# A small gate chain two tiles later, a cleared buffer moved into a loop step, and attention scores of two heads at a time

## The chip, the cores and the metric

The kernel runs on one core of one Trainium2 chip. The metric is the device time of one execution in microseconds. TensorE (PE in the profile) multiplies matrices into PSUM; VectorE (DVE), ScalarE (ACT) and GpSimd (POOL) work on the data between the multiplications; SyncE (SP) issues most transfers. Each engine runs its own list of instructions in order, and the lists meet at semaphores: an instruction can raise one, and another engine waits until it has reached a number.

## The reference

Two transformer blocks over 256 tokens of width 1024, with a context of 256 more tokens. All is float32. Cut to what the change touches:

```
# block 1, layer 0: gated delta rule on h @ w_in (q, k, v after a convolution), plus a gated MLP
log_alpha = -exp(a_log) * softplus(alpha_raw + dt_bias)      # per token, direction, head
gcum      = cumsum(log_alpha within a chunk)
decay     = exp(gcum_i - gcum_j), a_mat = strict_tril((beta k) k^T * decay)
t_mat     = inverse(I + a_mat)      # u = t_mat @ (beta v), w = t_mat @ (beta k exp(gcum)), then a scan

# block 1, layer 1: multi-head latent attention, 8 heads, 512 keys (256 of context, 256 own)
s = qn_h @ kn_h^T + qr_h @ kr^T     # 128 wide per head, and 64 wide with rotary, kr shared
p = softmax(s * 192**-0.5);  o_h = p @ v_h;  y = concat(o) @ w_out
```

Other layers (a convolutional MLP, a second block with three more attentions) are not changed.

## The kernel before

**Weights and tiles.** All weights pass through one stream of blocks of 128 x 1024. A block is split into a high and a low part: ScalarE makes the high one (`split`, line 1563), VectorE the low one (`low`, line 2060), and PE multiplies high x high, high x low and low x high (`mm3`, lines 646 to 648). A tile (`tile`) is 24 matmuls of 512 columns in this stage and 256 later. Two PSUM banks (PL[0], PL[1]) alternate for its results; six more (BK[0] to BK[5]) serve the small products. In the input stage block n is tile n; step t of ScalarE and VectorE handles block t + 2, and ScalarE can split block t + 2 only when PE has ended tile t (two buffers). Beside it, VectorE multiplies the rows of the modulation weights (`mod_tile`, line 2191, two passes of 1024 elements a step).

**The gate chain.** Tile 12 holds the raw gates of all tokens. From step 12 on, a chain goes through four engines, each step of it written by hand at a given step t of each engine's loop `for t in range(GATES, 25)`:
- ScalarE, t = 12 (`gate_rows`): bias, sigmoid, abs, exp and log on 8 rows, then the logarithm of the lengths of q and k (L2, read from BK[4], `l2_log`).
- VectorE, t = 13: gate rows (lines 2230, 2231, `g_soft`). PE, after tile 13: four transposes (line 778).
- VectorE, t = 14: copy to GTOK (line 2234, `g_tok`). PE, after tile 14: cumulative sums into BK[5] (lines 786, 787, `g_cs`).
- VectorE, t = 15: log factors (lines 2239 to 2248, `g_cum`). ScalarE, t = 15: exponential (line 1716, `g_exp`).
- PE, after tiles 15 and 16: `key_products` of the first stream's two token tiles (lines 768, 769; the second writes BK[4] and BK[5]).
- VectorE, t = 16: factors times beta (lines 2252, 2253, `g_fac`), for which PE waits after its second key products.
- After tiles 17, 19, 21, 23 (`ROWS_AT`): `rows` on PE (lines 760, 761), `decays` (2207) and `triangles` (2215 to 2222) on VectorE, two exponentials on ScalarE (1696, 1699), and a product on GpSimd (`decayed`, 1456). `rows` of one q waits until the triangles and exponentials before it are done.

**The inverse.** After the loop come 28 steps k for each of the two streams (`LEVELS`: 7 levels x 4 quarters). A step is a masked block on GpSimd (line 1476, `lev_ct`), a first product on PE (893 or 900), a copy on ScalarE (1770), a second product (917, 920) and a subtraction on VectorE (2351 to 2364). VectorE starts it with `first_u` (2330), after its last low part. Before the steps GpSimd clears the buffer TU (line 1461) when all modulation products of the stage are done; TU is first written by VectorE at the sixth level. At k = 8, 9, 10 GpSimd also issues three small transfers.

**The first attention** (`attend` with the layer MLA) has 16 items, head h and query tile qt. PE's step a is: scores of item a into one of three banks, transposes of item a - 2 (line 1140), values of item a - 3 (line 1189, into BK[4 + h % 2]). The scores are one product of all 128 rows of the array (line 1184) and one rotary product of 64 rows (line 1185), rows 0 to 63 for even heads and 64 to 127 for odd ones. A float32 product shows as two matmul instructions. VectorE's step is: reduce and scale item a, normalise item a - 1, and after every second item (`per` = 2, `lag` = 5) the low part of a finished head. ScalarE's step is: exponential of item a, copy of the transposes of item a - 2, high part of a finished head. The projection `out1` follows and takes the heads as its eight chunks.

Of the kernel before, what the change touches and what calls it, by code (L numbers as in the profile page):

```python
# [24 lines left out]
P = 128  # L25
# [259 lines left out]
def two_blocks_kernel(nc, x_in, mem_in, a_head, a_stream, cond_rows, w_stream, cols, gdn_tables, late_tables, ident, ws_t, bs_row, ln_rows, w_uk, w_uv, out):  # L285
# [4 lines left out]
    with ctx:  # L290
# [240 lines left out]
        class Layer:  # L531
            def __init__(self, name, heads, key_tiles, per_group, a0, e0, scale):
                self.name, self.heads, self.kt, self.per, self.a0, self.e0 = name, heads, key_tiles, per_group, a0, e0
                self.n, self.scale = 2 * heads, scale
                self.banks = [BK[0], BK[1], PL[0]]
                self.lag = per_group + 3
                self.steps = self.n - per_group + self.lag + 1
# [9 lines left out]

        MLA = Layer("mla", 8, 4, 2, 0, 0, 192 ** -0.5)
        DIL = PairLayer("dil", 16, 8, 64 ** -0.5)
        DSA = PairLayer("dsa", 24, 10, 96 ** -0.5)  # L550
        CRS = Layer("cross", 4, 2, 2, 32, 12, 256 ** -0.5)
        LAT = slice(SEQ, T2)
# [47 lines left out]
        GATES, UV_AT, GATE_AT = 12, 13, 21  # L600
        ROWS_AT = {17: 0, 19: 1, 21: 2, 23: 3}

# [39 lines left out]
        def _(pe):  # L642
# [130 lines left out]
            for t in range(GATES, 25):  # L773
                tile(t, t, slice(0, T2), T2)
                if t == 13:
                    pe.wait_ge(G["g_soft"], 1)
                    for x in range(4):
                        last = nc.tensor.transpose(BK[0][:, 40 * x:40 * x + 40], GT[0:40, x * P:(x + 1) * P], ID[0:40, 0:40])
                    last.then_inc(G["g_tr"], 1)
                if t == 14:  # L780
                    pe.wait_ge(G["g_tok"], 1)
                    pe.wait_ge(gdn_in, 16)
                    for d in range(2):
                        o = BK[5][:, 0:64].rearrange("p (t d r) -> p t d r", t=4, d=2)[:, :, d, :]
                        g = GTOK[:, :, 4 * d:4 * d + 4]
                        mm(o[:, :, 0:4], gtab("cum", d), g, start=True, stop=True)
                        last = mm(o[:, :, 4:8], ONES[:], g, start=True, stop=True)
                    last.then_inc(G["g_cs"], 1)
                if t == 15:
                    pe.wait_ge(silu_done, 8)  # L790
                    key_products(0, 0)
                if t == 16:
                    pe.wait_ge(G["g_cum"], 1)
                    key_products(0, 1)
                    pe.wait_ge(G["g_fac"], 1)
                if t in ROWS_AT:
                    rows(0, ROWS_AT[t])
# [70 lines left out]
            for st in range(2):  # L868
                if st:
# [8 lines left out]
                pe.wait_ge(G["gb_at"], 4 * st + 3)  # L878
                pe.wait_ge(G["gb_e"], 14 if st else 8)
# [247 lines left out]
            def attend(ly, scores, values):  # L1127

                nb = len(ly.banks)
                for a in range(ly.n + 3):  # L1130
                    if a < ly.n:
                        if ly.a0 or a >= nb:

                            pe.wait_ge(A["at_p"], ly.a0 + max(0, a - nb + 1))
                        scores(a // 2, a % 2, ly.banks[a % nb]).then_inc(A["at_s"], 1)
                    if 2 <= a < ly.n + 2:
# [5 lines left out]
                    if a >= 3:  # L1142
# [3 lines left out]
                        if p % ly.per == 0 and ly.e0 + e >= 2:  # L1146
                            pe.wait_ge(A["at_y"], ly.e0 + e - 1)
                        values(p // 2, p % 2, PT[:, p % 2, :, :]).then_inc(A["at_o"], 1)

# [31 lines left out]

            def mla_scores(h, qt, o):
                q, po = slice(qt * P, (qt + 1) * P), 64 * (h % 2)
                mm(o[:], MQ[:, h, q], KN[:, h, :], start=True, stop=False)
                return mm(o[:], MQ[po:po + 64, 8 + h // 2, q], KR[po:po + 64, :], start=False, stop=True)  # L1185

            def mla_values(h, qt, pt):
                for k in range(4):
                    last = mm(BK[4 + h % 2][:, qt * P:(qt + 1) * P], VT[:, k, h * P:(h + 1) * P], pt[:, k, :], start=(k == 0), stop=(k == 3))  # L1189
                return last  # L1190

            attend(MLA, mla_scores, mla_values)
            project("out1", LAT, SEQ, lambda k: (A["at_y"], k + 1))
            norm("n2_1")
# [229 lines left out]
        def _(pool):  # L1424
# [33 lines left out]
            for q in range(4):  # L1458
                decayed(0, q)
            pool.wait_ge(m_acc, 2 + 2 * MOD_IN)  # L1460
            nc.gpsimd.memset(TU[:], 0.0).then_inc(G["u_zero"], 1)
            for st in range(2):
# [3 lines left out]
                for k, (lev, q) in enumerate(LEVELS):  # L1466
# [79 lines left out]
        def _(act):  # L1546
# [154 lines left out]
            for t in range(GATES, 25):  # L1701
# [12 lines left out]
                if t == 15:  # L1714
                    act.wait_ge(G["g_cum"], 1)
# [188 lines left out]
            def attend(ly, out_bank, out_chunks):  # L1904
                for a in range(ly.steps):
                    w = ly.kt * P
                    if a < ly.n:
                        r = a % 3
                        act.wait_ge(A["at_m"], ly.a0 + a + 1)
                        if ly.a0 + a >= 3:  # L1910
                            act.wait_ge(A["at_t"], ly.a0 + max(0, a - 2))
                        f(PB[:, r, 0:w], ly.banks[r][:, 0:w], ACT.Exp, scale=STD[:, 10 + a % 2:11 + a % 2] if ly is CRS else ly.scale, bias=SM[:, 20 + r:21 + r], accum_out=SM[:, 24 + r:25 + r]).then_inc(A["at_p"], 1)
                    if 2 <= a < ly.n + 2:
# [38 lines left out]

            attend(MLA, lambda e: BK[4 + e % 2][:, 0:SEQ], lambda h, e: h[:, e, LAT])
            residuals("out1", 1, "n2_1")
# [90 lines left out]
        def _(dve):  # L2045
# [179 lines left out]
            for t in range(GATES, 24):  # L2225
                low(t + 2)
                if t == 13:
# [4 lines left out]
                if t == 14:  # L2232
                    dve.wait_ge(G["g_tr"], 1)
                    v.tensor_copy(GTOK[:], BK[0][:, 0:160].rearrange("p (t r) -> p t r", t=4)).then_inc(G["g_tok"], 1)
                if t == 15:
                    cum, total = GC[:, :, :, 0:4], GC[:, :, :, 4:8]
# [4 lines left out]
                    dve.wait_ge(G["g_cs"], 1)  # L2241
                    link(v.tensor_copy(GC[:], BK[5][:, 0:64].rearrange("p (t d r) -> p t d r", t=4, d=2)))
                    v.tensor_tensor(RP[:], cum, by_q, ALU.add)
# [4 lines left out]
                    v.tensor_tensor(BR, by_k, by_q, ALU.subtract).then_inc(G["g_cum"], 1)  # L2248
                if t == 16:
                    beta = GTOK[:, :, 32:40].rearrange("p t (d h) -> p t d h", d=2)  # L2250
# [284 lines left out]
            def attend(ly, out_bank, out_chunks):  # L2535
                for a in range(ly.steps):
                    w = ly.kt * P
                    if a < ly.n:
                        r = a % 3
                        dve.wait_ge(A["at_s"], ly.a0 + a + 1)  # L2540
                        link(v.tensor_reduce(SM[:, 16 + r:17 + r], ly.banks[r][:, 0:w], AXES.X, ALU.max))
                        if ly is CRS:
# [33 lines left out]

            attend(MLA, lambda e: BK[4 + e % 2][:, 0:SEQ], lambda h, e: h[:, e, LAT])
            project("out1", SEQ, 8)
# [146 lines left out]
```

## Time and profile before

| | |
|---|---|
| median of 3 runs | 1704.24 us (1702.66 to 1706.44) |
| profiled execution, whole | 1709.05 us |
| its span (first to last instruction) | 1707.2 us |
| mean granted PE clock | 0.96 |
| busy: PE, DVE, ACT, POOL | 1585.0 (93%), 1142.9 (67%), 787.8 (46%), 115.0 (7%) |
| chain that ended last, by engine | PE 79%, DVE 11%, ACT 5%, issue 3% |
| DMA | 230.50 MB, mean 135 GB/s |

The profile is of one execution, and its times run from the start of its span. Busy time of PE is modelled: a matmul's shown time reaches past the start of the next one, so the spacing of starts is the time that it costs. "Idle before" is time in which an engine stood still ahead of an instruction, with the instruction that released it. A row with "x8" merges eight instructions.

### The profile page before, as it was taken

What the parts mean: (1) busy time and instruction counts of PE and PEld (TensorE: products, weight loads), DVE (VectorE), ACT (ScalarE), POOL (GpSimd) and SP (SyncE); (2) the same over time, 40 slices, a digit from 0 to 9 for tenths busy, and PEclk for the clock granted to TensorE, in tenths of its full rate; (3) what the DMA queues carried; (4) which work ended last, traced back from release to release, by engine and by line L of the source; (5) the groups of instructions that cost most, each with busy time, mean ns of one, the idle gap of its engine ahead of it and who ended that gap; (6) DMA issues with size and microseconds to landing.
All of it is one profiled execution on the core that took longest, in us unless ns stands there. A gap on an engine that the chain in (4) does not pass through costs nothing.

```text
span 1707.2 us, 30981 instructions
## 1 busy us (share of the span) xinstructions
PE 1585.0 (93%) x11422; PEld 1387.1 (81%) x11422; DVE 1142.9 (67%) x1917; ACT 787.8 (46%) x1421; POOL 115.0 (7%) x130
## 2 busy tenths in 40 slices
PE   5997978889999999999999999999999988999998
PEld 2786868788777777788787589999898768999997
DVE  5974755554499999967455558885565665477653
ACT  3644533132354544432256447775444445566532
POOL 2000032220200000001000010001000001010000
PEclk9998988898999999999999999999899999999999
DMA  8343330000245555554432034556443222355552
GB/s 352 128 172 117 131 118 3 1 3 1 99 136 184 184 184 185 185 181 165 147 119 87 25 99 148 184 186 214 162 166 136 99 75 87 112 173 184 185 189 94
DMA packets 62906, 230.50 MB, mean 135 GB/s; under 512 B 6816, under 2 KB 8096, under 8 KB 62304
## 3 DMA queue, kind: packets, MB, share of 16 engines
q1 hardware_dynamic: 61408, 223.37, 38.4%
q0 software_dynamic: 1120, 5.54, 1.0%
q8 instruction: 64, 1.05, 0.3%
q10 hardware_dynamic: 288, 0.33, 0.1%
q14 instruction: 26, 0.21, 0.0%
HBM read 228.17 MB, written 1.05 MB: 134 GB/s over the span
## 4 chain that ended last, share of the span: by engine, by line
PE 79%; DVE 11%; ACT 5%; issue 3%; POOL 1%; DMA 1%; DVEq 0%; ACTq 0%; POOLq 0%
PE proj L646 21%; PE proj L648 20%; PE proj L647 20%; DVE w_low L2060 2%; PE bank L698 1%; ACT w_high L1563 1%; PE bank L900 1%; PE bank L917 1%; PE bank L1189 1%; PE bank L920 1%; DVE conv_mid L2140 1%; PE bank L1185 1%; PE proj L1101 1%; DMA ident_sb<-ident 1%; PE bank L948 1%
## 5 line engine op out<-in xcount | busy, mean ns | idle before, releaser
L646 PE MATMUL proj<-h_high,w_high 128*128 128x256 f32 (+1 forms) x1768 | 585.0, 331 | 23.2 <-DVE h_low L2093 14.0
L648 PE MATMUL proj<-h_high,w_low 128*128 128x256 f32 (+1 forms) x1768 | 572.2, 324 | 0.0
L647 PE MATMUL proj<-h_low,w_high 128*128 128x256 f32 (+1 forms) x1768 | 571.8, 323 | 0.0
L2060 DVE TENSOR_TENSOR w_low<-w_raw,w_high 128x1024 fp32r<-128x1024 f32 x322 | 393.3, 1224 | 197.9 <-ACT w_high L1563 196.5
L1563 ACT ACTIVATE w_high<-w_raw 128x1024 fp32r<-128x1024 f32 x322 | 338.1, 1054 | 251.7 <-PE proj L648 246.3
L646 PEld LDWEIGHTS proj<-h_high,w_high 128*128 128x128 f32 x1768 | 337.3, 191 | 65.9 <-issue 18.1
L648 PEld LDWEIGHTS proj<-h_high,w_low 128*128 128x128 f32 x1768 | 337.6, 191 | 27.3
L647 PEld LDWEIGHTS proj<-h_low,w_high 128*128 128x128 f32 x1768 | 337.3, 191 | 25.5
L646 PE MATMUL proj<-act_high,w_high 128*128 128x256 f32 (+1 forms) x608 | 190.1, 313 | 0.4 <-DVE w_low L2060 0.4
L647 PE MATMUL proj<-act_low,w_high 128*128 128x256 f32 (+1 forms) x608 | 189.9, 312 | 0.0
L648 PE MATMUL proj<-act_high,w_low 128*128 128x256 f32 (+1 forms) x608 | 188.9, 311 | 0.0
L646 PEld LDWEIGHTS proj<-act_high,w_high 128*128 128x128 f32 x608 | 114.1, 188 | 8.5 <-DVE w_low L2060 0.8
L648 PEld LDWEIGHTS proj<-act_high,w_low 128*128 128x128 f32 x608 | 114.3, 188 | 7.4
L647 PEld LDWEIGHTS proj<-act_low,w_high 128*128 128x128 f32 x608 | 113.9, 187 | 6.6
L1642 ACT ACTIVATE conv_in<-proj 128x512 f32<-128x512 f32 (+1 forms) x100 | 49.8, 498 | 120.5 <-PE proj L648 117.5
L2191 DVE SCALAR_TENSOR_TENSOR mod_products<-a_ring,cond_rows 128x1024 f32<-128x1024 f32 x80 | 103.0, 1287 | 0.1
L1441 POOL TENSOR_TENSOR tmp<-tmp 128x256 f32<-128x256 f32 (+1 forms) x40 | 43.7, 1099 | 806.3 <-ACT tmp L1579 627.9
L2191 DVE SCALAR_TENSOR_TENSOR a_ring<-a_ring,cond_rows 128x1024 f32<-128x1024 f32 x80 | 97.6, 1220 | 0.0
L2142 DVE SCALAR_TENSOR_TENSOR conv_mid<-conv_in,cols_sb,conv_mid 128x512 f32<-128x512 f32 (+1 forms) x100 | 63.5, 635 | 14.0 <-DVE conv_mid L2140 8.2
L2140 DVE SCALAR_TENSOR_TENSOR conv_mid<-conv_in,cols_sb,conv_mid 128x512 f32<-128x512 f32 (+1 forms) x100 | 63.3, 633 | 12.1 <-ACT conv_mid L1643 9.7
L1643 ACT ACTIVATE conv_mid<-proj,cols_sb 128x512 f32<-128x512 f32 (+1 forms) x100 | 58.8, 588 | 0.0
L1770 ACT ACTIVATE lev_m<-bank 128x256 f32<-128x256 f32 (+1 forms) x48 | 18.3, 383 | 84.6 <-PE bank L900 71.8
(406 smaller groups left out, 1939.2 us busy)
## 6 DMA issues: line engine op xcount, KB each, us to landing
w_raw<-w_stream SPq DMA_DIRECT2D x322, 512.0 KB, 3.3
a_ring<-a_stream SPq DMA_DIRECT2D x80, 512.0 KB, 3.2
a_first<-a_head SPq DMA_DIRECT2D x4, 1024.0 KB, 17.9
a_first<-a_stream SPq DMA_DIRECT2D x4, 1024.0 KB, 18.5
x<-x_in SPq DMA_DIRECT2D x1, 2048.0 KB, 10.6
late_tab<-late_tables POOLq DMA_DIRECT2D x1, 1408.0 KB, 6.6
cond_rows<-cond_rows SPq DMA_DIRECT2D x1, 1024.0 KB, 5.9
cond_rows<-cond_rows POOLq DMA_DIRECT2D x1, 1024.0 KB, 5.0
```

The source lines that it names most:

```text
L646: mm(out_, wh, xh, start=first, stop=False)
L647: mm(out_, wh, xl, start=False, stop=False)
L648: return mm(out_, wl, xh, start=False, stop=last)
L1441: nc.gpsimd.tensor_tensor(squares(name, 0), squares(name, 0), squares(name, k), ALU.add).then_inc(n_early, 1)
L1563: f(wh(n), RAW[:, n % 4, :], ACT.Copy).then_inc(w_high, 1)
L1642: f(XP[:, k % 2, 0:n, 1:SEQ + 1], PL[t % 2][:, 0:width].rearrange("p (s t) -> p s t", s=n), ACT.Copy)
L1643: f(C1[:, k % 2, 0:width], PL[t % 2][:, 0:width], ACT.Identity, scale=C[:, ds(taps + 3 * k + 1 + 3 * per * it, 1)]).then_inc(tile_out, 1)
L1770: f(M1[x, k % 2, :, :], BK[k % 2][x, 0:4 * 64].rearrange("p (h j) -> p h j", h=HEADS), ACT.Copy).then_inc(G["lv_m1"], 1)
L2060: v.tensor_tensor(wl(n), RAW[:, n % 4, :], wh(n), ALU.subtract).then_inc(w_low, 1)
L2140: v.scalar_tensor_tensor(o, XP[:, k % 2, 0:n, 0:SEQ], C[:, ds(taps + 3 * k + 3 * per * it, 1)], o, ALU.mult, ALU.add).then_inc(conv_mid, 1)
L2142: v.scalar_tensor_tensor(o, XP[:, k % 2, 0:n, 2:SEQ + 2], C[:, ds(taps + 3 * k + 2 + 3 * per * it, 1)], o, ALU.mult, ALU.add).then_inc(con ...
L2191: v.scalar_tensor_tensor(o, w, 1.0, cond[:, s, :], ALU.mult, ALU.mult, accum_out=MODF[:, ds(2 * (A_FIRST + j) + s + 2 * off, 1)]).then_inc ...
```

## The change

Three edits.

1. PE's key products come after tiles 13 and 14 (the second waits for `l2_log`, since it writes the bank that ScalarE reads the lengths from). The transposes come after tile 15, the sums after tile 16 (now in BK[1]), the wait for the factors after tile 18; the rows after 18, 20, 22 and 23. VectorE's gate rows are at t = 14, its copy at 16, its log factors at 17, its products with beta at 18; ScalarE's exponential at 17. Before the first stream's inverse PE waits for all four triangles, not three.
2. GpSimd clears TU at k = 8 of the first stream's inverse.
3. The attention MLA takes two heads' scores for one query tile in an even step: four full-height instructions, then the rotary ones of both heads. It has four score banks (PL[1] added); items are ordered head, head + 1 for one query tile, then for the other; outputs leave in groups of four items (`per` = 4, `lag` = 7) as 512 columns for two heads, and the later counts (`e0`) follow.

```diff
-        ROWS_AT = {17: 0, 19: 1, 21: 2, 23: 3}
+        ROWS_AT = {18: 0, 20: 1, 22: 2, 23: 3}
...
                 if t == 13:
+                    pe.wait_ge(silu_done, 8)
+                    key_products(0, 0)
+                if t == 14:
+                    pe.wait_ge(G["l2_log"], 1)
+                    key_products(0, 1)
+                if t == 15:
                     pe.wait_ge(G["g_soft"], 1)
...
-                if t == 14:
+                if t == 16:
                     pe.wait_ge(G["g_tok"], 1)
...
-                if t == 15:
-                    pe.wait_ge(silu_done, 8)
-                    key_products(0, 0)
-                if t == 16:
-                    pe.wait_ge(G["g_cum"], 1)
-                    key_products(0, 1)
+                if t == 18:
                     pe.wait_ge(G["g_fac"], 1)
...
-            pool.wait_ge(m_acc, 2 + 2 * MOD_IN)
-            nc.gpsimd.memset(TU[:], 0.0).then_inc(G["u_zero"], 1)
...
                     if st == 0 and k == 8:
+                        pool.wait_ge(m_acc, 2 + 2 * MOD_IN)
+                        nc.gpsimd.memset(TU[:], 0.0).then_inc(G["u_zero"], 1)
...
-        MLA = Layer("mla", 8, 4, 2, 0, 0, 192 ** -0.5)
+        MLA = Layer("mla", 8, 4, 4, 0, 0, 192 ** -0.5)
...
-                        if ly.a0 or a >= nb:
+                        if ly is MLA and a % 2 == 0:
+                            if a >= nb:
+                                pe.wait_ge(A["at_p"], a - nb + 2)
+                            scores(a, ly.banks[a % nb:a % nb + 2])
...
+            def mla_scores(a, banks):
+                h, qt = a // 4 * 2, a // 2 % 2
+                q = slice(qt * P, (qt + 1) * P)
+                for i, o in enumerate(banks):
+                    mm(o[:], MQ[:, h + i, q], KN[:, h + i, :], start=True, stop=False)
+                for i, o in enumerate(banks):
+                    mm(o[:], MQ[HALVES[i], 8 + h // 2, q], KR[HALVES[i], :], start=False, stop=True).then_inc(A["at_s"], 1)
```

## Rows read from the trace of the kernel before

**Rows 1.** Timeline of PE: start us, us, instruction [idle us before <- released by], its four waits.
```profile
140.81 0.65 PE L778 MATMUL bank<-ident_sb,gate_t 40*128 40x40 f32 x4 [6.75 <-DVE gate_t L2231]
...
151.31 0.57 PE L786 MATMUL bank<-g_tok,gdn_tab 128*128 128x16 f32 x2 [2.70 <-DVE g_tok L2234]
...
171.15 0.50 PE L646 MATMUL proj<-h_high,w_high 128*128 128x512 f32 x1 [0.88 <-DVE factors L2253]
...
227.04 4.01 PE L893 MATMUL bank<-ident_sb,lev_ct 64*64 64x64 f32 x64 [4.47 <-POOL lev_ct L1476]
```

**Rows 2.** Two windows: length, busy PE, granted clock, DMA share, GB/s.
```profile
151.30:158.20 6.90, 6.89 (x20) 0.51 0.41 152
...
250.40:253.40 3.00, 3.00 (x64) 0.50 0.02 5
```

**Rows 3.** Timeline of PE: first and second key products, tile 16 between them.
```profile
161.01 0.39 PE L768 MATMUL bank<-qkv 128*128 128x128 f32 x2
...
162.72 0.48 PE L646 MATMUL proj<-h_high,w_high 128*128 128x512 f32 x1
...
168.31 0.39 PE L768 MATMUL bank<-qkv 128*128 128x128 f32 x2
```

**Rows 4.** Timelines of ScalarE and VectorE: lengths' logarithm, copy of g_tok, factors.
```profile
137.17 0.29 ACT L1707 ACTIVATE qk_lengths<-bank,cols_sb 128x32 f32<-128x32 f32 x1
...
150.94 0.32 DVE L2234 COPY g_tok<-bank 128x160 f32<-128x160 f32 x1
...
170.91 0.18 DVE L2253 TENSOR_TENSOR factors<-factors,g_tok 128x32 f32<-128x32 f32 x1
```

**Rows 5.** Timelines of VectorE and GpSimd around the start of the inverse.
```profile
221.97 1.23 DVE L2191 SCALAR_TENSOR_TENSOR mod_products<-a_ring,cond_rows 128x1024 f32<-128x1024 f32 x1
...
224.72 1.22 DVE L2060 TENSOR_TENSOR w_low<-w_raw,w_high 128x1024 fp32r<-128x1024 f32 x1
226.93 1.27 DVE L2330 TENSOR_TENSOR inv_u_halves<-gdn_tab,lev_ct 128x256 f32<-128x256 f32 x2 [0.99 <-POOL lev_ct L1476]
...
224.40 1.80 POOL L1461 MEMSET inv_u<- 128x2048 f32 x1 [3.16 <-DVE a_ring L2191]
...
236.59 0.59 POOL L1482 DMA_DIRECT2D ln_rows_sb<-ln_rows  x1
241.77 0.72 POOL L1476 TENSOR_TENSOR lev_ct<-a_halves,gdn_tab 128x256 f32<-128x256 f32 x1 [4.58 <-PE bank L900]
```

**Rows 6.** Timeline of PE: first attention's start, one step of it, the projection behind it.
```profile
939.34 1.12 PE L1184 MATMUL bank<-mla_k,mla_q 128*128 128x512 f32 x2 [1.31 <-DVE kr L2528]
...
952.95 1.02 PE L1184 MATMUL proj<-mla_k,mla_q 128*128 128x512 f32 x2
953.90 1.12 PE L1185 MATMUL proj<-kr,mla_q 64*128 64x512 f32 x2
954.96 0.66 PE L1140 MATMUL bank<-ident_sb,probs 128*128 128x128 f32 x4
...
956.34 1.02 PE L1184 MATMUL bank<-mla_k,mla_q 128*128 128x512 f32 x2
...
994.81 0.36 PE L646 MATMUL proj<-h_high,w_high 128*128 128x256 f32 x1
```

**Rows 7.** Line 1185 (rotary products): ns minimum/median/maximum, first and last start.
```profile
L1185 PEld LDWEIGHTS bank<-kr,mla_q x22: 182/184/186, 940.4 to 987.9; 64*128 64x128 f32 x22
L1185 PE MATMUL bank<-kr,mla_q x22: 589/641/693, 940.4 to 988.4; 64*128 64x512 f32 x22
```

**Rows 8.** Timeline of PE: index scores (L1228, halves alternate), dilated scores (L1211, one half).
```profile
1315.72 0.70 PE L1228 MATMUL bank<-proj 64*128 64x256 f32 x4
...
1335.75 1.13 PE L1211 MATMUL bank<-proj 64*128 64x256 f32 x4
```

**Rows 9.** Groups by line, 939 to 995: busy us, mean ns | idle before.
```profile
L2541 DVE TENSOR_REDUCE small<-bank 128x1 f32<-128x512 f32 x11 | 7.6, 692 | 13.3 <-PE bank L1185 13.3
...
L1912 ACT ACTIVATE probs<-bank,small 128x512 f32<-128x512 f32 x11 | 7.6, 687 | 21.7 <-DVE small L2545 21.7
```

More of the change, by code:

```diff
@@ L534, in __init__ @@
                 self.n, self.scale = 2 * heads, scale
-                self.banks = [BK[0], BK[1], PL[0]]
+                self.banks = [BK[0], BK[1], PL[0]] if name == "cross" else [BK[0], BK[1], PL[0], PL[1]]
                 self.lag = per_group + 3
@@ L546, in __init__ @@
                 self.pairs = [(0, 4), (1, 5), (2, 6), (3, 7)] if name == "dsa" else [(0, 2), (1, 3), (4, 6), (5, 7)]
[L548 to L551 removed]
+        MLA = Layer("mla", 8, 4, 4, 0, 0, 192 ** -0.5)
+        DIL = PairLayer("dil", 16, 4, 64 ** -0.5)
+        DSA = PairLayer("dsa", 24, 6, 96 ** -0.5)
+        CRS = Layer("cross", 4, 2, 2, 32, 8, 256 ** -0.5)
         LAT = slice(SEQ, T2)
@@ L1131, in attend @@
                     if a < ly.n:
-                        if ly.a0 or a >= nb:
+                        if ly is MLA and a % 2 == 0:
+                            if a >= nb:
+                                pe.wait_ge(A["at_p"], a - nb + 2)
+                            scores(a, ly.banks[a % nb:a % nb + 2])
+                        elif ly is not MLA:
                             pe.wait_ge(A["at_p"], ly.a0 + max(0, a - nb + 1))
-                        scores(a // 2, a % 2, ly.banks[a % nb]).then_inc(A["at_s"], 1)
+                            scores(a // 2, a % 2, ly.banks[a % nb]).then_inc(A["at_s"], 1)
                     if 2 <= a < ly.n + 2:
@@ L1147, in attend @@
                             pe.wait_ge(A["at_y"], ly.e0 + e - 1)
-                        values(p // 2, p % 2, PT[:, p % 2, :, :]).then_inc(A["at_o"], 1)
+                        h, qt = (p // 4 * 2 + p % 2, p // 2 % 2) if ly is MLA else (p // 2, p % 2)
+                        values(h, qt, PT[:, p % 2, :, :]).then_inc(A["at_o"], 1)
             def pair_step(ly, a, scores, values):
@@ L1180, in pair_step @@
                     last.then_inc(A["at_o"], 1)
[L1182 to L1185, printed above, removed]
+            def mla_scores(a, banks):
[5 more added lines that the diff above has]
+                    mm(o[:], MQ[HALVES[i], 8 + h // 2, q], KR[HALVES[i], :], start=False, stop=True).then_inc(A["at_s"], 1)
             def mla_values(h, qt, pt):
+                at = h % 2 * SEQ + qt * P
                 for k in range(4):
-                    last = mm(BK[4 + h % 2][:, qt * P:(qt + 1) * P], VT[:, k, h * P:(h + 1) * P], pt[:, k, :], start=(k == 0), stop=(k == 3))
+                    last = mm(BK[4 + h // 2 % 2][:, at:at + P], VT[:, k, h * P:(h + 1) * P], pt[:, k, :], start=(k == 0), stop=(k == 3))
                 return last
             attend(MLA, mla_scores, mla_values)
-            project("out1", LAT, SEQ, lambda k: (A["at_y"], k + 1))
+            project("out1", LAT, SEQ, lambda k: (A["at_y"], k // 2 + 1))
             norm("n2_1")
@@ L1911, in attend @@
                             act.wait_ge(A["at_t"], ly.a0 + max(0, a - 2))
-                        f(PB[:, r, 0:w], ly.banks[r][:, 0:w], ACT.Exp, scale=STD[:, 10 + a % 2:11 + a % 2] if ly is CRS else ly.scale, bias=SM[:, 20 + r:21 + r], accum_out=SM[:, 24 + r:25 + r]).then_inc(A["at_p"], 1)
+                        f(PB[:, r, 0:w], ly.banks[a % len(ly.banks)][:, 0:w], ACT.Exp, scale=STD[:, 10 + a % 2:11 + a % 2] if ly is CRS else ly.scale, bias=SM[:, 20 + r:21 + r], accum_out=SM[:, 24 + r:25 + r]).then_inc(A["at_p"], 1)
                     if 2 <= a < ly.n + 2:
@@ L2226, in _ @@
                 low(t + 2)
-                if t == 13:
+                if t == 14:
                     dve.wait_ge(G["g_in"], 1)
@@ L2540, in attend @@
                         dve.wait_ge(A["at_s"], ly.a0 + a + 1)
-                        link(v.tensor_reduce(SM[:, 16 + r:17 + r], ly.banks[r][:, 0:w], AXES.X, ALU.max))
+                        link(v.tensor_reduce(SM[:, 16 + r:17 + r], ly.banks[a % len(ly.banks)][:, 0:w], AXES.X, ALU.max))
                         if ly is CRS:
```

18 lines of the change are left out of this document (9 added, 9 removed).

## The prediction

> **What bounds the kernel now.** I read the page first: TensorE (PE) is busy for 93% of the span and makes up 79% of the chain that ended last, so a change pays where PE waits, runs at the low clock, or has work that can go away. Then I read PE's waits in the timeline of the two stretches that the diff touches. From the end of input tile 13 to the first level product of the scan PE waits four times: 6.8 us for the gate rows before the transposes, 2.7 us for g_tok before the cumulative sums, 0.9 us for the factors before tile 17, and 4.5 us for GpSimd's first masked block [rows 1]. The granted clock comes next: after the 2.7 us wait it is 0.51 for 6.9 us, the lower level (1.2 GHz), and after another wait of 2.6 us elsewhere 0.50 for 3.0 us [rows 2]. In the first attention there is no wait to remove: PE repeats the same step every 3.39 us (952.95 to 956.34) without a gap, so only its own work counts there, 55.47 us from 939.34 to 994.81 [rows 6].
>
> **Change 1, the gate chain two tiles later.** PE's own work in the stretch stays: eleven tiles, four groups of rows, two groups of key products, four transposes, four sums. From 162.72 to 168.31 a tile is 5.59 us at the high clock, and from 161.01 to 162.72 a group of 16 small matmuls 1.71 us [rows 3]. What moves is where PE meets the other engines.
> - Before the transposes (6.75 us now). VectorE made the gate rows after weight block 15, whose split ScalarE could only do after its own gate work. The key products come forward to steps 13 and 14. The first needs only conv outputs made long before. Tile 13 ended at 134.06 (140.81 less 6.75) [rows 1], so they run to 135.8, tile 14 to 141.4, the second group to 143.1, tile 15 to 148.7. The second group waits for the logarithm of the lengths, which ScalarE started at 137.17 for 0.29 us [rows 4]: over by then. The gate rows wait only for block 16, whose split starts when tile 14 ends: about 145. So this wait goes, cover 3.7 us. Nothing is late behind it.
> - Before the sums (2.70 us). This one stays. The copy of g_tok stands on VectorE behind the low part of the block two tiles on, and that block can only be split once PE has ended the tile just run. The rows show it: tile 14 ends at 148.61 (151.31 less 2.70), the copy ran from 150.94 for 0.32 us [rows 1, 4]. At step 16 the same order holds: 2.7 us again.
> - Before the factors (0.88 us). The factors were ready at 171.09 (170.91 plus 0.18), 2.8 us after tile 16 had given way to the key products at 168.31 [rows 3, 4]. Those products covered 1.7 us of it. They are gone from this place, and nothing replaces them: with the tail of the last matmul counted as busy, 2.7 us are exposed at step 18. This edit loses 1.8 us by itself.
> Waits: 6.75 + 2.70 + 0.88 = 10.3 now, 2.7 + 2.7 = 5.4 after: 4.9 us less.
> - Clock. From 140.81 to 148.61 PE needed 7.8 us for transposes and a tile worth 6.0 (5.59 and an estimate of 0.4 for the transposes and switches); from 151.31 to 161.01 9.7 us for sums and a tile worth 6.4 (5.59 + half of the sums' 1.70): 5.1 us lost to the low clock. After: the first wait should repeat the loss that follows it now, 3.3. The second is bounded by the two windows: half of 3.4 us (the 3.0 of the row and its edges) up to half of 6.9, or nothing if the clock holds. I take 1.7, since dense products follow it. Loss 5.0, a gain of 0.1; ends +5.1 and -1.8.
> The stretch gives 5.0 us, ends 3.1 and 10.0. Rows now come at 18, 20, 22 and 23; the third and fourth have only one tile between them. The fourth waits for the third's triangles, which end 6.9 us after a tile's end (the modulation pass behind them starts at 221.97, and tile 23 ended at about 215.1, that is 222.57 less 1.71 less 5.59, less tails) [rows 3, 5]; the rows and the tile between take 7.3 us, so I cost it at nothing, with 0.4 us of cover. If the cover fails, PE stalls by the difference.
>
> **Change 2, clearing the half-block buffer in step 8.** GpSimd now clears it from 224.40 for 1.80 us, after the last modulation product, and VectorE then stands idle 0.99 us for the first masked block [rows 5]. In step 8 the clearing lies between 236.59 plus 0.59 and the next masked block at 241.77 [rows 5]: 4.6 us of GpSimd's waiting hide 1.8. Without that cover it would cost at most 1.8. VectorE's split of block 26 beside today's clearing took its usual 1.22 us, so I expect no slowing of the neighbour. With the clearing gone, the first two masked blocks and products can run before VectorE is free. But VectorE gets later: step 22's two modulation products and block 25 now stand before step 23's decays, by my working about 0.7 us. Today it is free at 225.9 (224.72 + 1.22), 3.4 us after tile 24's end at 222.57; then at 4.1, against 4.4 with the wait for GpSimd. The four first products run 4.0 us at the low clock [rows 1]; two of them leave the path, less the masked block that the third waits for. I take 1.0 us of gain, between -0.7 (VectorE's lateness alone) and 2.5 (two products and the head start).
>
> **Change 3, scores of two heads at a time.** A step now is 0.95 us of full-height products (952.95 to 953.90), 1.06 of half-height rope products, and 1.38 of transposes and values [rows 6]. A pair's four full-height instructions take 1.81 (0.43 each, one change of arrangement instead of two). Its four rope instructions use both halves of the array and two banks. Nothing in this attention shows that; the index scores do: four instructions on alternating halves take 0.70 us, four of equal width on one half 1.13 [rows 8], so they run two by two (the busy time runs 0.17 us past the point at which the next operation starts: 0.53 against 0.96). For 512 columns that makes 1.06 a pair instead of 2.12. PE's work per pair falls from 6.79 to 1.81 + 1.06 + 2.76 = 5.63.
> Not all of it is kept. VectorE's order is reduce(a), then normalise(a-1). The odd item's normalising stands behind the reduce of the next pair, which starts only after all eight score instructions. The reduce takes 0.69, ScalarE's exponential, which goes before the transposed copy, 0.69 [rows 9]; the small operations and handovers come to that. Laid out item by item, PE waits 0.2 us for the odd transposes and 0.3 us for the values in each pair (6.16 a pair), 1.1 us at the start and 1.0 at the end. The stretch comes to 50.7 us; the same laying out gives 55.4 for the kernel before (55.47 in the trace). Gain 4.7. The wider copies (one for two heads) are behind the last values: the projection has 30 matmuls before it needs chunks 6 and 7, so they are hidden; uncovered, they cost 1.5. Ends: 2.2 if the rope products don't overlap, 9.2 if no wait appears (8 x 1.16).
>
> The Trainium skill speaks against the size: "TensorE: Matmul & The Clock Gate", Part 3, section on the mechanism, says that matmuls start and end in strict program order and only weight loads of another row group run ahead. By it the second head's first product could not start before the first head's second, and the four would take about 1.5 us. The trace disagrees (0.70 against 1.13 above) [rows 8]. The sum would hardly move: the reduce comes earlier for the first head, the waits shrink, and the stretch comes to 50.9.
>
> **The sum.** 5.0 + 1.0 + 4.7 = 10.7 us. The profiled execution took 1709.05 (span 1707.2), 4.8 above the median of the runs shown; taken off it, 1698.3, and off the median of 1704.24, 1693.5. The rest is the same work with the same waits.
>
> **Rivals.**
> - The clock holds through both 2.7 us waits. The loss of 5.0 goes, 1688.5. For it: the 0.9 us wait had no low clock behind it. Against: both waits of this size in rows 2 had one. 15%.
> - The attention gives less: the rope products run one after another. Then 2.2 instead of 4.7, 1696. For it: the operands are accumulated here, in the index scores they are not. 12%.
> - The change doesn't do what it says: the wait at the transposes is not the gate rows' lateness but comes back whole two tiles on, or at step 18 and 23, with its clock. Then the stretch gives 0, 1698.5. For it: two of three waits do come back. Against: the 6.75 came from ScalarE's gate work, which is done once, at 137. 7%.
> - Slower: each rope instruction empties the array before the next, since the half changes within a pair. One alone takes 0.69 us, and its weight load 0.18 [rows 7]; four then take 3.5, a pair 1.81 + 3.5 + 2.76 = 8.1 instead of 6.79, eight pairs 10.2 more. With the other 6.0 gained: 1708.4. It decides the sign once the four take over 4.02 - 1.81 + 6.0/8 = 2.96 us. Against: four on alternating halves took 0.70 us in the index scores [rows 8]. 3%.
> My forecast has 63%.
>
> **The numbers.** 1693.5 is the likeliest. Downwards the clock rival (1688.5) and the upper end of the attention reach to about 1686.5; upwards the rivals at 1696 and 1698.5 to 1699.5. About what a measurement of this kernel can tell from no change is 0.2%, 3.4 us. Only the slower rival, and a return of the waits together with a weak attention, miss that: faster 0.93, same 0.04, slower 0.03.
>
> **What would show it.** PE's waits after the change: none at the transposes, one of 2.7 us for g_tok after tile 16, one of about 2.7 for the factors after tile 18, a low clock behind each; the rows after tile 23 without a wait; GpSimd's masked blocks 0 and 1 before VectorE's block 26 has ended; the clearing between masked blocks 8 and 9 with PE's products unmoved. In the attention: pairs every 6.2 us, four rope instructions in 1.1, waits of 0.2 and 0.3 on normalise and on the transposed copy. I am wrong if the waits at steps 16 and 18 are absent or over 4 us, if the rope four take over 1.5, or if tile 24 or the first products wait longer than now.

## The result, and the profile after

The changed kernel took 1694.11 us (median of 5 runs, 1690.71 to 1695.20) against 1704.12 for the kernel before (5 runs, 1700.29 to 1706.44): ratio 0.9934, 95% interval 0.9916 to 0.9952. Forecast: 1693.5, range 1686.5 to 1699.5. Its profiled execution has a span of 1692.0 us, 15.2 less than the 1707.2 of before; only 11.6 of these lie in the code that the change touches.

I cut every span at the same places: the end of input tile 13, the end of tile 24, the first value transposes of the scan, the first score product of the first attention, and the first product of the projection behind it [rows 6]. Us:

| stretch | before | after | after, second profile |
|---|---|---|---|
| start to tile 13's end | 134.1 | 135.5 | 134.2 |
| tiles 14 to 24, with the gate chain | 88.5 | 81.8 | 81.8 |
| start of the scan | 8.4 | 8.0 | 8.0 |
| scan and projections (unchanged code) | 708.4 | 707.9 | 706.5 |
| first attention | 55.5 | 50.9 | 50.9 |
| to the end (unchanged code) | 712.4 | 707.9 | 712.1 |

The timeline of PE after, tile 14 to the scan (start us, us, instruction, in brackets the idle time before it and who ended it), answers [rows 1]:

```profile
150.00 0.43 PE L784 MATMUL bank<-ident_sb,gate_t 40*128 40x40 f32 x4
...
158.84 0.56 PE L792 MATMUL bank<-g_tok,gdn_tab 128*128 128x16 f32 x2 [2.70 <-DVE g_tok L2242]
...
176.87 0.49 PE L760 MATMUL bank<-ident_sb,log_rows 128*128 128x128 f32 x2 [2.67 <-DVE factors L2261]
...
217.99 1.15 PE L894 MATMUL bank<-ident_sb,lev_ct 64*64 64x64 f32 x32 [0.69 <-ACT gate L1721]
...
223.40 1.97 PE L894 MATMUL bank<-ident_sb,lev_ct 64*64 64x64 f32 x32 [4.26 <-POOL lev_ct L1483]
```

No wait at the transposes, one of 2.70 and one of 2.67: all three are as forecast. The 0.69 us ahead of the first two level products, ended by ScalarE (line 1721), is new; the next two products wait for VectorE and GpSimd all the same. The two windows behind them (length; busy us and instructions of PE, PEld, DVE, ACT and POOL; granted clock, DMA share, GB/s) answer [rows 2]:

```profile
158.80:165.70 6.90, 6.86 (x20) 5.79 (x21) 2.27 (x4) 0.00 (x0) 0.00 (x0) 0.51 0.44 163
176.80:189.70 12.90, 12.83 (x64) 10.89 (x65) 9.40 (x19) 5.81 (x7) 1.29 (x1) 1.00 0.36 135
```

The lower level (1.2 GHz) behind the first, none behind the second. VectorE and GpSimd at the end of tile 24 (217.30), which answer [rows 5]:

```profile
217.60 1.75 DVE L2199 SCALAR_TENSOR_TENSOR mod_products<-a_ring,cond_rows 128x1024 f32<-128x1024 f32 x1
...
220.87 1.22 DVE L2068 TENSOR_TENSOR w_low<-w_raw,w_high 128x1024 fp32r<-128x1024 f32 x1
222.01 0.75 DVE L2338 TENSOR_TENSOR inv_u_halves<-gdn_tab,lev_ct 128x256 f32<-128x256 f32 x2
```

```profile
216.85 1.42 POOL L1483 TENSOR_TENSOR lev_ct<-a_halves,gdn_tab 128x256 f32<-128x256 f32 x2
...
230.73 1.81 POOL L1488 MEMSET inv_u<- 128x2048 f32 x1
232.48 0.59 POOL L1490 DMA_DIRECT2D ln_rows_sb<-ln_rows  x1
```

The masked blocks come before VectorE is free and its 0.99 us wait is gone; the clearing lies where nobody waits for it. But VectorE is free 4.7 us after tile 24's end (222.01), and its pass beside the masked blocks takes 1.75 us instead of 1.22, although they share only 0.67 us of it (217.60 to 218.27). A pair of the attention on PE answers [rows 6]:

```profile
948.62 1.88 PE L1191 MATMUL proj<-mla_k,mla_q 128*128 128x512 f32 x4
950.44 1.13 PE L1193 MATMUL proj<-kr,mla_q 64*128 64x512 f32 x4
951.50 0.66 PE L1144 MATMUL bank<-ident_sb,probs 128*128 128x128 f32 x4
951.99 1.06 PE L1198 MATMUL bank<-probs_t,mla_v 128*128 128x128 f32 x8
953.12 0.66 PE L1144 MATMUL bank<-ident_sb,probs 128*128 128x128 f32 x4
953.83 1.16 PE L1198 MATMUL bank<-probs_t,mla_v 128*128 128x128 f32 x8
954.83 1.45 PE L1191 MATMUL bank<-mla_k,mla_q 128*128 128x512 f32 x3
```

A pair every 6.21 us (948.62 to 954.83), 1.82 of full-height products and 1.06 for the four rope (rotary) products, where two took 1.06 before.

### The profile page after: what moved, and what is told of

It reads as the page before. It is cut to its first block, busy times and chain, and to the rows that moved or that the text cites. A ratio compares the mean times of both kernels' runs of the same rounds, so it can differ in the third digit from the quotient of the medians.

```text
span 1692.0 us, 30969 instructions
## 1 busy us (share of the span) xinstructions
PE 1572.8 (93%) x11422; PEld 1380.7 (82%) x11422; DVE 1141.4 (67%) x1913; ACT 786.4 (46%) x1416; POOL 115.2 (7%) x130
## 3 DMA queue, kind: packets, MB, share of 16 engines
q8 instruction: 64, 1.05, 0.3%
HBM read 228.17 MB, written 1.05 MB: 135 GB/s over the span
## 4 chain that ended last, share of the span: by engine, by line
PE 79%; DVE 11%; ACT 5%; issue 3%; POOL 1%; DMA 1%; DVEq 0%; ACTq 0%; POOLq 0%
PE proj L646 21%; PE proj L648 20%; PE proj L647 20%; DVE w_low L2068 2%; PE bank L698 1%; ACT w_high L1571 1%; PE bank L901 1%; PE bank L918 1%; PE bank L1198 1%; PE bank L921 1%; DVE conv_mid L2148 1%; DMA ident_sb<-ident 1%; PE bank L949 1%; PE proj L1102 1%; DVE mod_products L2199 1%
```

## The experiments

In all of them the ratio is to the kernel before, run on the same chip in turns, with its 95% interval.

**Each edit alone, and the sum.** gate_only has only the two-tile move of the gate chain, on all engines:

```diff
-                if t == 14:
+                if t == 16:
...
-        ROWS_AT = {17: 0, 19: 1, 21: 2, 23: 3}
+        ROWS_AT = {18: 0, 20: 1, 22: 2, 23: 3}
```

> The kernel before with the gate chain's two-tile move alone (clearing and attention as before). My theory of the change: two TensorE waits of 2.7 us in place of waits of 6.75, 2.70 and 0.88 us, 4.9 us less waiting, and one fall of the clock in place of one and a half. The profile after showed no fall behind the second wait (tiles 13 to 24 6.7 us shorter, not 5.0). So: 5.0 us faster if the clock falls after the second wait in most executions, 6.7 us if it mostly stays up, 0.993 to 0.997 times the time before to say it as a band of -10 to -5 us with noise. Rival, that the gain of the change lies elsewhere (in the attention, or in drift of unchanged code): 0 to -2 us.

1698.28 us, ratio 0.9948 (0.9932 to 0.9965). Tiles 14 to 24 take 82.0 us, 6.5 less; but the scan's start takes 9.3, 0.9 more. The gain is there, at a cost behind it. clear_only has the clearing's move, and with it PE's wait for all four triangles (VectorE's work), which the change lists under its first edit and gate_only leaves out:

```diff
-            pool.wait_ge(m_acc, 2 + 2 * MOD_IN)
-            nc.gpsimd.memset(TU[:], 0.0).then_inc(G["u_zero"], 1)
...
+                        pool.wait_ge(m_acc, 2 + 2 * MOD_IN)
+                        nc.gpsimd.memset(TU[:], 0.0).then_inc(G["u_zero"], 1)
```

> The kernel before with the clearing of the half-block buffer moved into step 8 alone (and the wait on GpSimd's blocks that goes with it). My theory: the 0.99 us that VectorE waited at 226.93 for GpSimd's masked blocks goes, time 1.0 us less, which lies at the limit of what five rounds can tell. Rival A, the one that the pair of profiles suggests: only 0.4 us, since VectorE's pass beside GpSimd's earlier masked blocks takes 1.75 us instead of 1.22. Rival B, nothing, since the log decays end last there in any case: the wait is seen on VectorE for another cause, time the same. In the profile: the idle time ahead of the pass at 226.93 and the duration of the passes on L2192 tell them apart.

1704.25 us, ratio 0.9988 (0.9977 to 0.9999). The start of the scan takes 7.1 us instead of 8.4: 1.3 less, more than I expected even though the pass on VectorE takes 1.75 us here too. 9.3 without and 8.0 with the clearing, beside the moved chain, is 1.3 again. So the clearing gives 1.3, and what made the pair of profiles show only 0.4 was the gate chain, not the clearing. Rivals A and B fall. attn_only has only the pairs of heads:

```diff
-            def mla_scores(h, qt, o):
+            def mla_scores(a, banks):
...
-        MLA = Layer("mla", 8, 4, 2, 0, 0, 192 ** -0.5)
+        MLA = Layer("mla", 8, 4, 4, 0, 0, 192 ** -0.5)
```

> The kernel before with the first attention's pairs of heads alone. My theory: the attention takes 50.7 to 50.9 us in place of 55.5, the time falls by 4.7 us, all of it inside the attention; four rope products in 1.06 us, a pair every 6.2 us. Rival, that the code after the attention gains too (the pair of profiles shows 4.5 us there, in unchanged code): 9 us less, and the stretch from the attention's end to the end of the kernel shorter than 712 us in this profile and in the ratio. Rival, that the attention's gain is drawn from a clock that happened to be high: under 2.5 us.

1699.49 us, ratio 0.9963 (0.9949 to 0.9977). The attention takes 50.92 us, and the code behind it 712.8: no gain there. The first rival falls; the 4.5 us that the pair of profiles showed behind the attention isn't the change's. And the sum, the changed kernel again with no edit:

> The changed kernel itself, once more, as the sum to which the three single edits must add: by the theory 5.0 to 6.7 + 0.4 to 1.0 + 4.7, so 10 to 12.4 us less than before. Its profile is a second draw of the clock: by the theory (the clock's fall after a wait of 1.7 to 2.7 us varies between executions) the granted clock behind the second wait of step 18, and behind the 1.70 us wait at 1282.65, may stand at 0.5 this time, with the waits themselves the same to 0.2 us. Rival (the clock is settled by the code alone): both windows read 1.00 again.

1692.37 us, ratio 0.9921 (0.9905 to 0.9936). By the medians the three edits gave 7.2 + 1.2 + 6.0 = 14.4 and together 13.1; by the stretches 6.5 - 0.9, 1.3 and 4.6, 11.5 together, and the changed kernel has 11.6. Waits are the same to 0.01 us, the clock behind them is not. The two windows of its second profile:

```profile
157.60:161.60 4.00, 4.00 (x15) 3.42 (x16) 2.17 (x4) 0.00 (x0) 0.00 (x0) 0.57 0.26 85
175.60:178.80 3.20, 3.20 (x11) 2.70 (x11) 1.37 (x5) 0.97 (x3) 0.00 (x0) 0.52 0.09 36
```

A shorter fall behind the first wait, and one behind the second. "Settled by the code alone" falls.

**Where the attention's gain comes from.** serial_rope takes one line out of the changed kernel, so that the two halves' products aren't neighbours:

```diff
                     mm(o[:], MQ[:, h + i, q], KN[:, h + i, :], start=True, stop=False)
-                for i, o in enumerate(banks):
                     mm(o[:], MQ[HALVES[i], 8 + h // 2, q], KR[HALVES[i], :], start=False, stop=True).then_inc(A["at_s"], 1)
```

> The changed kernel, but each head's rope product directly behind its own full-height product, so that the two half-height products of a pair are no longer next to each other. Nothing else differs: same pairs, banks and waits. My theory (the gain of the attention comes from the two halves of the array running at once): four half-height instructions take about 2.0 us again instead of 1.06, and as VectorE and ScalarE hide part of it the attention comes to 53 to 53.5 us (50.93 in the changed kernel, 55.47 before), the time 2.2 to 2.6 us more than the changed kernel, 0.993 becoming 0.9945 to 0.995. Rival, that the pairing matters through the fewer changes of arrangement and the fourth bank: the attention stays at 51 us, the time as in the changed kernel.

1700.01 us, ratio 0.9958 (0.9942 to 0.9973). The attention takes 55.78 us, 0.3 more than before the change. A pair on PE:

```profile
940.23 1.02 PE L1191 MATMUL bank<-mla_k,mla_q 128*128 128x512 f32 x2
941.18 1.12 PE L1192 MATMUL bank<-kr,mla_q 64*128 64x512 f32 x2
942.24 1.13 PE L1191 MATMUL bank<-mla_k,mla_q 128*128 128x512 f32 x2
943.29 1.12 PE L1192 MATMUL bank<-kr,mla_q 64*128 64x512 f32 x2
944.34 0.66 PE L1144 MATMUL bank<-ident_sb,probs 128*128 128x128 f32 x4
...
947.06 1.02 PE L1191 MATMUL proj<-mla_k,mla_q 128*128 128x512 f32 x2
```

The four rope products take 1.06 + 1.05 us instead of 1.06. PE within the first 0.4 us of a pair's rope products, in the changed kernel (950.45 to 950.90) and in this one (941.30 to 941.60):

```profile
950.44 0.70 PE L1193 MATMUL proj<-kr,mla_q 64*128 64x512 f32 x2
```

```profile
941.18 0.69 PE L1192 MATMUL bank<-kr,mla_q 64*128 64x512 f32 x1
```

Two run at once in the first, one in the second. With the halves apart nothing of the attention's gain is left, so the fourth bank and the new order of items alone give none. The size that I expected was wrong. A pair takes 6.83 us with no idle time in it, 1.24 more than PE's own 5.59 (normalise_two, below): 1.05 from the rope products and 0.19 from the full-height ones (0.95 + 1.06 instead of 1.82). Half of the 1.24 is hidden, since a pair of the changed kernel holds 0.62 us of waiting (6.21 less 5.59). The other 0.62, eight times, is the loss of 4.9 us; I had expected 2.3.

normalise_two leaves PE's order alone and changes the other two engines':

```diff
-                    if 1 <= a <= ly.n:
-                        p = a - 1
+                    for p in ([a - 1, a] if a % 2 else []) if ly is MLA and a <= ly.n else [a - 1] if 1 <= a <= ly.n else []:
```

and on ScalarE

```diff
+                    first = ly is MLA and a % 2 == 0 and 2 <= a < ly.n + 2
+                    if first:
+                        copies()  # the transposed probabilities, ahead of the exponential
...
-                    if 2 <= a < ly.n + 2:
+                    if 2 <= a < ly.n + 2 and not first:
```

> The changed kernel with another order of VectorE and ScalarE in the first attention: VectorE normalises both items of a pair in the odd step, and ScalarE's transposed copy goes ahead of the exponential in even steps. TensorE's instructions are the same. My theory (behind 1.81 + 1.06 + 2.76 = 5.63 us of TensorE's own work the rest of each pair's 6.2 us is two short waits for the normalised probabilities and for the transposed copy): by the same laying out, item by item, the attention takes 45.6 us instead of 50.9, the time 5 us less than the changed kernel. Rival A: the 0.57 us a pair is not these waits but TensorE's change between kinds of product, and the attention stays at 50 to 51 us. Rival B: normalising later makes ScalarE or VectorE the bound, and the pair takes over 6.2 us.

1690.06 us, ratio 0.9891 (0.9872 to 0.9910). The attention takes 45.46 us (45.6 expected), a pair 5.59:

```profile
940.26 1.88 PE L1191 MATMUL bank<-mla_k,mla_q 128*128 128x512 f32 x4
942.08 1.13 PE L1193 MATMUL bank<-kr,mla_q 64*128 64x512 f32 x4
943.14 0.66 PE L1144 MATMUL bank<-ident_sb,probs 128*128 128x128 f32 x4
...
945.85 1.88 PE L1191 MATMUL proj<-mla_k,mla_q 128*128 128x512 f32 x4
```

So the pair's 6.21 was PE's own 5.6 and the two waits, and both rivals fall. By time the gain is less sharp: against 0.9921 for the changed kernel in another series the ratio is 0.003 lower, about 5 us, but the two intervals overlap; the 5.5 us is read from the stretch.

**The two waits of the gate chain.** early_factors moves two pieces of VectorE's work ahead of the split of the weight block:

```diff
             for t in range(GATES, 24):
+                if t == 16:
+                    dve.wait_ge(G["g_tr"], 1)
+                    v.tensor_copy(GTOK[:], ...).then_inc(G["g_tok"], 1)
+                if t == 18:
+                    ...  # the two factor products of step 18
                 low(t + 2)
```

> The changed kernel with VectorE's copy of g_tok (step 16) and the last two factor products (step 18) placed ahead of the low part of the weight block two tiles on, instead of behind it. My theory (each 2.7 us wait is only this order on VectorE, since the block can't be split before TensorE has ended the tile just run): both waits go, 5.4 us, and with the first the low clock behind it, 3.4 us; tiles 13 to 24 take 73 to 74 us instead of 81.8 and the time is 8 to 9 us less than the changed kernel's, about 1684 to 1685. Rival A: only the waits go and the clock falls at the next wait instead, 5 us. Rival B: the waits are the late arrival of the chain itself (ScalarE's or VectorE's work of the step before), and moving the instruction leaves 1 to 2 us of each, or makes the low part late, with a new wait of TensorE on h_low or w_low: under 3 us.

1684.58 us, ratio 0.9872 (0.9855 to 0.9890). Tiles 14 to 24 take 73.6 us with no low clock in them. The first wait is gone; of the second 0.60 us is left. Rivals A and B fall. cover_factors moves PE's second key products to step 18:

```diff
-                if t == 14:
-                    pe.wait_ge(G["l2_log"], 1)
-                    key_products(0, 1)
...
                 if t == 18:
+                    pe.wait_ge(G["l2_log"], 1)
+                    key_products(0, 1)
                     pe.wait_ge(G["g_fac"], 1)
```

> The changed kernel with the second group of key products (1.7 us of small products on TensorE) in step 18, directly ahead of the sums that wait for the factors, instead of in step 14. My theory (the wait before the factors is 2.7 us because the key products that used to cover 1.8 of it were moved away): that wait shrinks to about 0.9 us, nothing else appears, tiles 13 to 24 take 80.0 us instead of 81.8. Rival: the second group is needed where it stands, for the rows of step 18 or as TensorE's cover in step 14, and a wait of the same size opens there: no gain. The size is at the limit of what five rounds tell (1.8 us is 0.1%); the trace decides.

1691.08 us, ratio 0.9904 (0.9888 to 0.9920). PE before the rows of step 18 (my expectation calls them sums):

```profile
172.28 0.49 PE L760 MATMUL bank<-ident_sb,log_rows 128*128 128x128 f32 x2 [0.89 <-DVE factors L2260]
```

0.89 instead of 2.67, and no new wait. The stretch is 78.6 and not 80.0 mostly because this execution lost only 1.7 us to the clock. Last, tok_early takes away the first wait only:

```diff
             for t in range(GATES, 24):
+                if t == 16:
+                    dve.wait_ge(G["g_tr"], 1)
+                    v.tensor_copy(GTOK[:], ...).then_inc(G["g_tok"], 1)
                 low(t + 2)
```

> The changed kernel with VectorE's copy of g_tok (step 16) alone placed ahead of the low part of the weight block; the factors of step 18 stay late. It asks why the clock did not fall behind the second 2.7 us wait: in four profiles with this gate chain it stayed at 1.00 there, while behind the first it read 0.51. Theory A, it depends on what came before (TensorE had just been through a wait and a stretch at the low clock): with the first wait gone the second becomes the first, and the low clock with its 1.7 to 3.4 us now lies behind step 18; tiles 13 to 24 take 81.8 - 2.7 = 79.1 us or 1.7 less. Theory B, the place in step 18 never brings a fall, whatever came before: no low clock between the tile 13 and tile 24, 81.8 - 2.7 - 3.4 = 75.7 us.

1687.17 us, ratio 0.9883 (0.9855 to 0.9910); 77.2 us from tile 13's end to tile 24's. The premise of this expectation was wrong. I had the sum of low clock over the stretch for four profiles, 3.4 us each time, and took it to lie behind the first wait; window by window it was 3.4 + 0 in two of them and 1.7 + 1.7 in the other two. So the experiment tells less than it should: the clock does fall in step 18 here,

```profile
150.00:168.00 18.00, 16.14 (x75) 13.05 (x73) 11.87 (x26) 6.43 (x8) 0.00 (x0) 1.00 0.39 138
168.80:172.30 3.50, 3.49 (x17) 3.50 (x18) 0.00 (x0) 1.68 (x2) 0.00 (x0) 0.54 0.53 217
```

which speaks against B, as the second profile of the changed kernel and gate_only had done already, but A isn't shown by it, since in those two it falls there with the first wait in place. What decides it stays open.

**The scan's start.** rows_21 gives back the distance between the last two groups of rows:

```diff
-        ROWS_AT = {18: 0, 20: 1, 22: 2, 23: 3}
+        ROWS_AT = {18: 0, 20: 1, 21: 2, 23: 3}
```

> The changed kernel with the third rows of decays in step 21 instead of 22, so that two tiles lie again between the third and the fourth, as in the kernel before. It asks what took 0.9 us of the scan's start (from tile 24's end to the first value transposes: 7.10 us with the clearing moved alone, 8.00 with the gate chain moved as well). My theory (VectorE comes 0.7 to 0.9 us later to the masked blocks, since the third rows' triangles, two modulation products and a weight block stand before the fourth's decays): 7.1 us again, the rest as in the changed kernel; 0.9 us of 1692, not to be told by the clock of the whole. Rival (the lateness comes from the chain's later end or from GpSimd's earlier masked blocks beside VectorE's pass, 1.75 us instead of 1.22): 8.0 us again. It may cost at the other end, where third and second rows now have one tile between: then TensorE waits before the rows of step 21, up to 1 us.

1690.98 us, ratio 0.9910 (0.9881 to 0.9939). The start of the scan takes 6.80 us instead of 8.00, and no wait appears before step 21. PE's last wait there and VectorE's pass:

```profile
214.76 1.75 DVE L2199 SCALAR_TENSOR_TENSOR mod_products<-a_ring,cond_rows 128x1024 f32<-128x1024 f32 x1
...
220.56 1.66 PE L894 MATMUL bank<-ident_sb,lev_ct 64*64 64x64 f32 x32 [3.37 <-POOL lev_ct L1483]
```

3.37 instead of 4.26: this 0.9 us is what the edit gives back. The pass still takes 1.75, so it isn't that: it is VectorE's queue of work between the third rows and the fourth. The other 0.3 us is the clock's and not the edit's. The two products behind the wait take 1.66 instead of 1.97, and in their first 0.90 us the granted clock reads 1.00 here (220.56 to 221.46) and 0.50 in the changed kernel (223.40 to 224.30).

**Together.** best_cover is the edits of early_factors, cover_factors and normalise_two on the changed kernel; best_rows adds that of rows_21. The edits are those shown above.

> Three of the earlier edits on the changed kernel at once: g_tok's copy and the factor products ahead of the low part, the second key products in step 18, and the first attention with both items normalised in the odd step. By the theory that these are separate waits they add: tiles 13 to 24 73.6 less the 0.6 us wait that was left at step 18, 73.0; attention 45.5; so 8.8 + 5.5 us less than the changed kernel, 1692.4 to 1694.1 becoming about 1678 to 1679.5, ratio to before about 0.984. Rival (part of the gain is handed back at a later wait or by the clock): over 1682.

> The same three edits, and the third rows in step 21. If the scan's start gains its 0.9 us, this kernel is about 0.9 us faster than the one with the three edits, within the noise; in the profile the stretch from tile 24's end to the value transposes is 7.1 us instead of 8.0. If the second and third rows crowd each other, a wait of up to 1 us appears ahead of step 21 or 22 and nothing is gained.

1680.13 us, ratio 0.9844 (0.9818 to 0.9869), and 1681.20, ratio 0.9836 (0.9811 to 0.9862): both beat the kernel before by about 25 us, and the changed one by 11 to 14 (medians of different series). best_cover came out 0.6 to 2.1 us above what was expected. best_rows should have been 0.9 below it and came out 1.1 above; the noise covers that. Both profiles had the long form of the last stretch (712.1 and 712.2 us, see the end). The two can't be told apart by time. By the stretches both have 72.7 for the tiles and 45.5 for the attention; the scan's start is 7.95 and 6.98. PE's waits in best_cover from 130 to 230 (total, times, longest):

```profile
PE bank L893 <- POOL lev_ct L1482: 4.2, 1, 4.2
PE proj L813 <- DVE k_decay L2286: 2.6, 1, 2.6
PE bank L893 <- ACT gate L1720: 0.7, 1, 0.7
```

Nothing is left of the gate chain. The 2.6 us stands in the scan of the kernel before too.

## Why the prediction was right, step by step

- Waits of the gate chain: right in place and size (none, 2.70, 2.67; forecast none, 2.7, 2.7), 4.9 us. That they are VectorE's order behind the weight block is shown by early_factors (all of the first, 2.07 of the second's 2.67), that the missing key products cost 1.8 by themselves by cover_factors.
- Clock: the term that was mis-sized. I took a loss of 5.0 after (3.3 + 1.7), so a gain of 0.1. Summed over windows of 1 us as one less the granted clock, the stretch lost 3.4 us in four profiles with both waits (3.4 + 0 in the changed kernel's first and in normalise_two, 1.7 + 1.7 in gate_only and the second) and 1.7 + 0 in two (serial_rope, rows_21); never 5.0. The rival in which the clock holds through both came in none. The stretch gave 6.7 us, in the two executions that lost least 8.1 and 8.3, where I had 5.0 with ends 3.1 and 10.0. By its own terms the clock's lower end was -1.65 (5.1 less 3.3 less half of 6.9), not -1.8, and the stretch's 3.25.
- Scan's start: forecast 1.0, measured 0.4. VectorE's lateness cost 0.9 and not the 0.7 that change 2 allowed for it (gate_only; rows_21 gets 0.9 back). The clearing's move gave 1.3, beside the old chain and beside the moved one alike, where the forecast of 1.0 took about 1.7 for it. I had expected no slowing of VectorE; its pass beside the masked blocks took 0.5 us longer. That is about the size of what is missing, but no run separates it. "I cost it at nothing, with 0.4 us of cover" held for PE before the rows of step 23. The clearing itself is hidden, as said.
- Attention: forecast 4.7 and 50.7 us, measured 4.5 and 50.93. Rope products two by two are shown by serial_rope, the two short waits by normalise_two.
- The Trainium skill ("TensorE: Matmul & The Clock Gate", Part 3, the mechanism) says that matmuls start and end in strict program order. From this I worked out about 1.5 us for the four rope instructions, taking each head's two instructions as separate entries of that order; that step is mine and not the page's. The same part also has several matmuls run at once in different tiles of the array, which the prediction left out. The trace agrees with the overlap and not with the 1.5: the four took 1.06 us, and 2.11 when the halves weren't neighbours.
- The rival in which the rope products run one after another was mispriced. It left 2.2 us of the attention's gain; serial_rope leaves nothing (55.78), in part because its full-height products are apart too.
- Sum: 11.6 by the stretches against 10.7 forecast; 10.0 and 13.1 by the medians of two comparisons. The terms' errors, +1.7, -0.6 and -0.2, partly cancel. That the median (1694.11) fell within 0.6 us of 1693.5 is therefore partly luck: the mechanism was right, the size of the clock term was not.

## What to carry to other kernels

When a wait moves with its chain, look at what stands ahead of the releasing instruction on its own engine: here moving the chain saved 4.9 us of waiting, and reordering two small pieces of VectorE's work another 8 us, of which 3.4 are the low clock behind the waits. A wait has two prices, its length and the low clock behind it, and the second differs from run to run, so it belongs in the range and not in the sum. Before two profiles are subtracted, cut both at the same places and look first at the stretches that nothing has changed.

## What the runs showed of the hardware that was not expected

The granted clock behind the same wait in the same code differs between executions. The stretch behind the first attention is unchanged in all kernels. In 7 of 14 profiles it took 712 to 713 us, in the other 7 707.7 to 709.0; the seven long ones, and none of the short ones, have a fall of the clock behind one wait of 1.70 us some 300 us into it. attn_only first, clear_only second, each with its wait and a window of 4.9 us behind it:

```profile
1288.08 1.01 PE L698 MATMUL bank<-ones,tmp 128*128 128x1 f32 x4 [1.70 <-ACT tmp L1587]
...
1289.60:1294.50 4.90, 4.90 (x14) 3.84 (x13) 0.88 (x3) 0.00 (x0) 0.00 (x0) 0.50 0.34 107
```

```profile
1293.88 0.61 PE L698 MATMUL bank<-ones,tmp 128*128 128x1 f32 x4 [1.70 <-ACT tmp L1578]
...
1295.15:1300.05 4.90, 4.90 (x26) 3.94 (x25) 2.60 (x7) 1.39 (x3) 0.00 (x0) 1.00 0.31 107
```

12 matmuls fewer in the same 4.9 us. The kernel before and the changed one fell on different sides, which is most of the 4.5 us that their profiles differ by there. What decides it in an execution stays open; no run here varied it.

A pass of VectorE over 1024 columns took 1.75 us where GpSimd's masked blocks overlap it, in clear_only, the changed kernel and rows_21 alike, and 1.23 where they don't (the kernel before, gate_only); beside GpSimd's clearing a split over as many columns took its usual 1.22 [rows 5].
